# Up projections of three feed-forward stages as pairs of 64-row products into two banks

## The chip, the cores and the metric

One core of one Trainium2 chip runs the whole kernel, one launch. The metric is the device time in microseconds. Engines are named as in the profile: PE is TensorE's matrix multiply, PEld its weight load, DVE is VectorE, ACT is ScalarE, POOL is GpSimd, SP is SyncE.

## The reference

The kernel computes two transformer blocks on 256 tokens of width 1024, batch 1. The part that the change touches is the feed-forward half step, which occurs four times:

```python
def swiglu_half_step(h, g, w1, w3, w2):
    u = rmsnorm(h, g)
    return h + FFN_HALF * ((jax.nn.silu(u @ w1) * (u @ w3)) @ w2)
```

Here `w1` and `w3` are 1024 by 2816 and `w2` is 2816 by 1024, all float32. Between these steps lie a Mamba-2 mixer, a sliding-window attention, and a second block with an RWKV and latent-attention mixer and a mixture of experts.

## The kernel before

The stages run one after the other: `ffn0`, `ssm`, `ffn1`, `ffn2`, `kv`, `attn`, `ffn3`, `rwkv`, `mla`, `mix`, `peer`. Each engine has its own instruction list, and semaphores order them.

**How a product is made.** Weights come as tiles of 128 by 1024 floats through four ring slots (`ring`). For each tile ACT writes `w_hi`, the tile rounded to float32r (`make_hi`, L304), and DVE writes `w_lo`, the remainder (`make_lo`, L309). The normed activations are held in the same way as `u_hi` and `u_lo`. A product is then three float32r passes, hi by hi, hi by lo and lo by hi (`passes`, L357), summed in PSUM. `project_split` does this over the `DC` = 8 chunks of the contraction: each matmul has a 128 by 128 piece of the weights as its stationary operand and 256 token columns as its moving operand, so one product is 24 matmuls.

**A feed-forward stage** has `FC` = 22 hidden chunks of 128. They are taken alternately as `b` = 0 and 1. For every chunk `up` makes two products, with `w1` and with `w3`, into the two halves of bank `UP[b]` (banks 4 and 5). ACT then does `silu` on the first half (L695), and DVE does `gate` (L717 to L720): two multiplications of silu by the second half of the bank, and a subtraction that gives `x_hi` and `x_lo`. `down` (`close_split`) multiplies `x_hi` and `x_lo` by the `w2` tile into the four accumulators `ACC` (banks 0 to 3), in 12 matmuls with 512 moving columns.

**Order on PE.** The first chunk's products are made by `project_first`, which isn't changed. After `clear_acc` a loop of ten iterations does `up(1, i)`, `down(0, i)`, `up(0, i + 1)`, `down(1, i)`, and behind the loop come `up(1)` of the last chunk, then three quarters of `down(0)`, three of `down(1)`, and the last quarter of each. So an up of chunk j+1 always runs before the down of chunk j, and the gate of chunk j has the down of j-1 and the up of j+1 as its cover. Only at the end is this otherwise: the last chunk's gate has only three quarters of one down.

**Order on ACT and DVE.** In an iteration ACT does `silu` of a chunk and then three `make_hi` (the next `w1`, `w3` and `w2` tiles, in that order), and DVE does `gate` and then three `make_lo`. Each of these waits for the semaphore of what it needs, in the order of the list. Behind the loop DVE does `gate(0)`, `make_lo` of the last `w2` tile, `lead_next` (the `make_lo` of the first tile of the next stage) and `gate(1)`.

**Banks 6 and 7** are `TP[0]` and `TP[1]`. The stages' norms turn their rows through them. In `ffn2`, named `HOLDS_KV`, they also serve the key and value work; in `ffn0`, `ffn1` and `ffn3` they are idle during the loop.

Other code that the prediction reads in the trace: L386 (`project`, plain float32 with 128 rows and 256 columns), L1255 and L1256 (`scores`: for each half `a` of the partitions, rows 0 to 63 or 64 to 127, one product of 128 and one of 256 columns, each half into a bank of its own), L1542 (`lora`: four products on rows 0 to 63, then four on rows 64 to 127) and L1590 (`tile64`: alternating 64 by 64 products on the two halves). All of these are plain float32, and the profile lists each of their matmuls as two records. A float32r matmul is one record.

Of the kernel before, what the change touches and what calls it, by code (L numbers as in the profile page):

```python
# [31 lines left out]
P = 128  # L32
# [173 lines left out]
def program(nc, io, stages=STAGES):  # L206
# [23 lines left out]
    def S(name):  # L230
        if name not in sems:
            sems[name] = ctx.enter_context(nc.semaphore(name))
        return sems[name]
# [4 lines left out]
    with ctx:  # L238
# [31 lines left out]
        def area(at, *shape):  # L270

            n = int(np.prod(shape))
            a = arena[:, at:at + n]
            if len(shape) == 2:
                a = a.rearrange("p (a b) -> p a b", a=shape[0])
            if len(shape) == 3:
                a = a.rearrange("p (a b c) -> p a b c", a=shape[0], b=shape[1])
            return a
# [22 lines left out]
        def make_hi(act, slot, stage, i, nth=0):  # L301
            act.wait_ge(full[slot], (use(stage, slot, i, nth) + 1) * 16)
            act.wait_ge(split_read[slot], use_split(stage, slot, i, nth) + 1)
            act.activation(w_hi[slot][:, :], ring[slot][:, :], ACT.Copy).then_inc(hi_made[slot], 1)  # L304

        def make_lo(dve, slot, stage, i, nth=0):

            dve.wait_ge(hi_made[slot], use_split(stage, slot, i, nth) + 1)
            dve.tensor_tensor(w_lo[slot][:, :], ring[slot][:, :], w_hi[slot][:, :].bitcast(F32),  # L309
                              ALU.subtract).then_inc(freed[slot], 1)  # L310
# [10 lines left out]
        def lead_next(dve, before):  # L321

            for stage in stages[stages.index(before) + 1:][:1]:
                lead_vector(dve, stage, slice(0, 1))

        def lead_next_hi(act, before):

            for stage in stages[stages.index(before) + 1:][:1]:
                lead_scalar(act, stage, slice(0, LEAD_BEFORE.get(stage, 0)))
# [20 lines left out]
        def split_done(eng, slot, stage, i, nth=0):  # L350

            eng.wait_ge(split_read[slot], use_split(stage, slot, i, nth) + 2)
# [8 lines left out]
        def project_split(pe, out, slot, stage, i, nth=0):  # L361
            multiplied(pe, slot, stage, i, nth)
            for c in range(DC):
                cols = slice(c * P, (c + 1) * P)
                mm = passes(pe, out, (w_hi[slot][:, cols], w_lo[slot][:, cols]), (u_hi[:, c, :], u_lo[:, c, :]),
                            c == 0, c == DC - 1)
            return mm.then_inc(split_read[slot], 1)

        def close_split(pe, b, slot, stage, i, last=False, quarters=range(4)):

            multiplied(pe, slot, stage, i)
            for q in quarters:
                rows, cols = slice((q // 2) * P, (q // 2 + 1) * P), slice((q % 2) * 512, (q % 2 + 1) * 512)
                mm = passes(pe, ACC[q][:, :], (x_hi[:, b, rows], x_lo[:, b, rows]),
                            (w_hi[slot][:, cols], w_lo[slot][:, cols]), False, last)
                if last and q < 3:
                    mm.then_inc(S("acc_done"), 1)
            if q == 3:
                mm.then_inc(split_read[slot], 1)
# [233 lines left out]

        silu_buf = area(4 * D, 2, T)
        hid_buf = area(4 * D + 2 * T, 2, T)

        def stage_of(k):
            return f"ffn{k}"  # L620
# [9 lines left out]
        def ffn_tile(kind, k, i, b):  # L630
            return (2 + b, f"ffn{k}", i, 0) if kind == 2 else (kind, f"ffn{k}", i, b)
# [21 lines left out]
        def ffn_tensor(pe, k, updates):  # L653
            stage = f"ffn{k}"
            base = FC * ffn_no[stage]

            def up(b, i):
                pe.wait_ge(S("hid_ready"), base + 2 * i + b + 1)
                for n in range(2):
                    project_split(pe, UP[b][:, n * T:(n + 1) * T], *ffn_tile(n, k, i, b))  # L660

            def down(b, i, last=False, quarters=range(4)):
                pe.wait_ge(S("hid_ready"), base + 2 * i + b + 3)
                close_split(pe, b, 2 + b, stage, i, last, quarters)

            pe.wait_ge(S("hid_ready"), base + 1)
            project_first(pe, stage, *((UP[0][:, n * T:(n + 1) * T], *ffn_tile(n, k, 0, 0)) for n in range(2)), one_bank=True)
            clear_acc(pe, updates)
            if stage == HOLDS_KV:
                pe.wait_ge(S("table_loaded"), 16)  # L670
                pe.wait_ge(S("rest_loaded"), 16)
                pe.matmul(TP[0][0:16, 0:384], rel[0:BUCKETS, :], C("onehot")[0:BUCKETS, :], start=True,
                          stop=True).then_inc(S("line_done"), 1)
            with pe.Fori(0, FC // 2 - 1) as i:
                up(1, i)
                down(0, i)
                up(0, i + 1)
                down(1, i)
            up(1, FC // 2 - 1)
            if stage == HOLDS_KV:  # L680
                pe.wait_ge(S("line_ready"), 1)
                kv_turn(pe, 0)
                kv_turn(pe, 1)
            down(0, FC // 2 - 1, quarters=range(3))
            if stage == HOLDS_KV:
                kv_turn(pe, 2)
                kv_turn(pe, 3)
            down(1, FC // 2 - 1, True, range(3))
            down(0, FC // 2 - 1, quarters=(3,))
            down(1, FC // 2 - 1, True, (3,))  # L690

        def ffn_scalar(act, k):
            def silu(b, i):
                split_done(act, *ffn_tile(1, k, i, b))
                act.activation(silu_buf[:, b, :], UP[b][:, 0:T], ACT.Silu).then_inc(S("silu_ready"), 1)  # L695

            act.preload_act_table(ACT.Silu)
            for kind in range(2):
                make_hi(act, *ffn_tile(kind, k, 0, 1))
            with act.Fori(0, FC // 2 - 1) as i:  # L700
                for b in range(2):
                    silu(b, i)
                    for kind, *at in ffn_next(k, i, b):
                        make_hi(act, *ffn_tile(kind, k, *at))
            silu(0, FC // 2 - 1)
            make_hi(act, *ffn_tile(2, k, FC // 2 - 1, 1))
            lead_next_hi(act, stage_of(k))
            silu(1, FC // 2 - 1)

        def ffn_vector(dve, k):  # L710
            stage = f"ffn{k}"
            base = FC * ffn_no[stage]

            def gate(b, i):
                dve.wait_ge(S("silu_ready"), base + 2 * i + b + 1)
                dve.wait_ge(split_read[2 + b], use_split(stage, 2 + b, i) + 1)
                dve.tensor_tensor(x_hi[:, b, :], silu_buf[:, b, :], UP[b][:, T:2 * T], ALU.mult)  # L717
                dve.tensor_tensor(hid_buf[:, b, :], silu_buf[:, b, :], UP[b][:, T:2 * T], ALU.mult)
                dve.drain()
                dve.tensor_tensor(x_lo[:, b, :], hid_buf[:, b, :], x_hi[:, b, :].bitcast(F32),  # L720
                                  ALU.subtract).then_inc(S("hid_ready"), 1)

            for kind in range(2):
                make_lo(dve, *ffn_tile(kind, k, 0, 1))
            if stage == HOLDS_KV:
                dve.wait_ge(S("line_done"), 1)
                dve.tensor_tensor(bias_line[0:16, :], TP[0][0:16, 0:384], C("outside")[0:16, :],
                                  ALU.add).then_inc(S("line_ready"), 1)
            with dve.Fori(0, FC // 2 - 1) as i:
                for b in range(2):  # L730
                    gate(b, i)
                    for kind, *at in ffn_next(k, i, b):
                        make_lo(dve, *ffn_tile(kind, k, *at))
            gate(0, FC // 2 - 1)
            make_lo(dve, *ffn_tile(2, k, FC // 2 - 1, 1))
            lead_next(dve, stage)
            gate(1, FC // 2 - 1)
            if stage == HOLDS_KV:
                for q in range(4):
                    dve.wait_ge(S("kv_turned"), q + 1)  # L740
                    dve.tensor_tensor(quarter(u_t, q), TP[q % 2][:, :].rearrange("p (c t) -> p c t", c=4),
                                      spread(V("g_kv", 4 * (q % 2), 4 * (q % 2) + 4), P), ALU.mult).then_inc(S("kv_made"), 1)
            update_h(dve, 0.5, upd[stage], stage)
# [2401 lines left out]
```

## Time and profile before

| | us |
|---|---|
| median of 2 runs | 2172.53 |
| lowest and highest | 2172.39, 2172.67 |
| profiled execution, its own time | 2173.42 |
| its span in the trace | 2171.2 |
| PE busy | 2133.1 (98%) |
| PEld busy | 1923.5 (89%) |
| DVE busy | 1450.1 (67%) |
| ACT busy | 1039.8 (48%) |

The trace's durations are summed against the span. The time of a run is about 2 us more than the span of the same execution (2173.42 against 2171.2), which lies around it, and the median is 0.9 us below the profiled execution.

A matmul's record lasts longer than the matmul keeps the array, since records overlap: what a stream of matmuls costs is the distance from one start to the next, got here by dividing a stretch by the count in it. "64*128 64x256" in a row is a product with 64 rows (contraction) and 128 stationary columns, whose moving operand is 64 by 256.

### The profile page before, as it was taken

What the parts mean: (1) busy time and instruction counts of PE and PEld (TensorE: products, weight loads), DVE (VectorE), ACT (ScalarE), POOL (GpSimd) and SP (SyncE); (2) the same over time, 40 slices, a digit from 0 to 9 for tenths busy, and PEclk for the clock granted to TensorE, in tenths of its full rate; (3) what the DMA queues carried; (4) which work ended last, traced back from release to release, by engine and by line L of the source; (5) the groups of instructions that cost most, each with busy time, mean ns of one, the idle gap of its engine ahead of it and who ended that gap; (6) DMA issues with size and microseconds to landing.
All of it is one profiled execution on the core that took longest, in us unless ns stands there. A gap on an engine that the chain in (4) does not pass through costs nothing.

```text
span 2171.2 us, 41978 instructions
## 1 busy us (share of the span) xinstructions
PE 2133.1 (98%) x15291; PEld 1923.5 (89%) x15291; DVE 1450.1 (67%) x2757; ACT 1039.8 (48%) x1766; POOL 104.0 (5%) x78
## 2 busy tenths in 40 slices
PE   9999999999999999999999899999999999999999
PEld 7999998899899987899899669889889999999998
DVE  5556998555565546655685578989886666666665
ACT  4335776433444336533562464458534444444443
POOL 0000000000000000000000004500000000000000
PEclk9999999999999999999999999999999999999999
DMA  6555664455566534455541034344677666665664
GB/s 216 186 187 173 206 194 134 159 187 188 174 207 207 189 131 131 166 188 186 184 146 54 21 117 147 117 169 146 212 228 237 207 204 204 210 185 185 190 185 135
DMA packets 107724, 374.23 MB, mean 172 GB/s; under 512 B 11984, under 2 KB 17888, under 8 KB 107376
## 3 DMA queue, kind: packets, MB, share of 16 engines
q1 hardware_dynamic: 102848, 355.01, 50.1%
q0 software_dynamic: 4784, 17.99, 2.8%
q8 instruction: 58, 0.95, 0.2%
q14 instruction: 34, 0.28, 0.0%
HBM read 362.41 MB, written 13.69 MB: 173 GB/s over the span
## 4 chain that ended last, share of the span: by engine, by line
PE 88%; DVE 6%; ACT 2%; DVEq 1%; DMA 1%; issue 1%; POOL 0%; ACTq 0%
PE bank L357 71%; PE bank L386 5%; PE bank L1590 3%; PE bank L2650 2%; DVE w_lo L309 1%; PE bank L563 1%; ACT w_hi L304 1%; DVE arena L2836 0%; DVE arena L2829 0%; PE bank L581 0%; PE bank L339 0%; DMA ring<-in_ssm_in 0%; DVE arena L2830 0%; PE bank L341 0%; PE bank L2174 0%
## 5 line engine op out<-in xcount | busy, mean ns | idle before, releaser
L309 DVE TENSOR_TENSOR w_lo<-ring,w_hi 128x1024 fp32r<-128x1024 f32 x575 | 695.0, 1222 | 410.9 <-ACT w_hi L304 408.9
L304 ACT ACTIVATE w_hi<-ring 128x1024 fp32r<-128x1024 f32 x599 | 624.6, 1056 | 631.1 <-PE bank L357 568.9
L357 PE MATMUL bank<-u_hi,w_hi 128*128 128x256 f32 x2712 | 771.4, 284 | 7.2 <-POOL w_lo L309 5.3
L357 PE MATMUL bank<-u_hi,w_lo 128*128 128x256 f32 x2712 | 767.4, 283 | 0.0
L357 PE MATMUL bank<-u_lo,w_hi 128*128 128x256 f32 x2712 | 767.3, 283 | 0.0
L357 PEld LDWEIGHTS bank<-u_hi,w_hi 128*128 128x128 f32 x2712 | 519.7, 192 | 19.3 <-issue 8.0
L357 PEld LDWEIGHTS bank<-u_lo,w_hi 128*128 128x128 f32 x2712 | 519.7, 192 | 7.5 <-issue 0.5
L357 PEld LDWEIGHTS bank<-u_hi,w_lo 128*128 128x128 f32 x2712 | 519.7, 192 | 0.0
L357 PE MATMUL bank<-w_hi,x_hi 128*128 128x512 f32 x992 | 390.8, 394 | 1.3 <-DVE x_lo L2158 0.9
L357 PE MATMUL bank<-w_lo,x_hi 128*128 128x512 f32 x992 | 388.3, 391 | 0.0
L357 PE MATMUL bank<-w_hi,x_lo 128*128 128x512 f32 x992 | 386.1, 389 | 0.0
L357 PEld LDWEIGHTS bank<-w_hi,x_lo 128*128 128x128 f32 x992 | 186.3, 188 | 40.5
L357 PEld LDWEIGHTS bank<-w_hi,x_hi 128*128 128x128 f32 x992 | 187.0, 188 | 39.2 <-DVE x_lo L2158 1.8
L357 PEld LDWEIGHTS bank<-w_lo,x_hi 128*128 128x128 f32 x992 | 187.0, 189 | 31.3
L386 PE MATMUL bank<-u_t,ring 128*128 128x256 f32 x640 | 145.3, 382 | 0.9 <-DVE u_t L520 0.7
L386 PEld LDWEIGHTS bank<-u_t,ring 128*128 128x128 f32 x640 | 119.6, 191 | 19.0 <-issue 1.3
L2901 DVE TENSOR_TENSOR x_hi<-arena 128x256 fp32r<-128x256 f32 (+1 forms) x128 | 54.4, 425 | 121.8 <-ACT arena L2745 111.4
L2745 ACT ACTIVATE arena<-bank 128x256 f32<-128x256 f32 x96 | 37.1, 386 | 176.8 <-PE bank L357 176.8
L309 POOL TENSOR_TENSOR w_lo<-ring,w_hi 128x1024 fp32r<-128x1024 f32 x24 | 56.9, 2384 | 1103.5 <-ACT w_hi L304 1095.5
L2650 PE MATMUL bank<-arena 128*128 128x128 f32 x512 | 63.1, 278 | 2.7 <-issue 1.7
L2650 PEld LDWEIGHTS bank<-arena 128*128 128x128 f32 x512 | 60.5, 191 | 5.8 <-issue 2.6
L1590 PE MATMUL bank<-arena 64*64 64x64 f32 (+1 forms) x1504 | 55.6, 228 | 7.1 <-ACT arena L1824 2.6
(316 smaller groups left out, 1793.5 us busy)
## 6 DMA issues: line engine op xcount, KB each, us to landing
ring<-in_w SPq DMA_DIRECT2D x264, 512.0 KB, 3.6
ring<-in_expert_u SPq DMA_DIRECT2D x128, 512.0 KB, 3.5
ring<-in_expert_v SPq DMA_DIRECT2D x128, 512.0 KB, 4.1
ring<-in_ssm_in SPq DMA_DIRECT2D x40, 512.0 KB, 4.3
gate_dram<-con SPq DMA_DIRECT2D x16, 576.0 KB, 2.8
arena<-gate_dram POOLq DMA_DIRECT2D x9, 1024.0 KB, 8.5
ring<-in_ssm_out SPq DMA_DIRECT2D x16, 512.0 KB, 4.2
ring<-in_w_o SPq DMA_DIRECT2D x16, 512.0 KB, 3.6
```

Source lines behind the costliest of these rows:

```text
L304: act.activation(w_hi[slot][:, :], ring[slot][:, :], ACT.Copy).then_inc(hi_made[slot], 1)
L309: dve.tensor_tensor(w_lo[slot][:, :], ring[slot][:, :], w_hi[slot][:, :].bitcast(F32), ALU.subtract).then_inc(freed[slot], 1)
L357: mm = pe.matmul(out, left[a], right[b], start=start and n == 0, stop=stop and n == 2, skip_group_check=True)
L386: mm = pe.matmul(out, ring[slot][:, c * width:(c + 1) * width], u_t[:, c, :], start=(c == 0), stop=(c == DC - 1))
L563: pe.matmul(bank[4][:, :], zeros[:, 0:P], zeros[:, :], start=True, stop=True)
L1590: mm = pe.matmul(bank[b][a, at:at + width], left[a, :], right[a, :], start=(n == 0), stop=(n == len(products) - 1))
L2650: mm = pe.matmul(ROT[g][:, t * P:(t + 1) * P], one_b[:, g, t, :], one_a[:, g, t, :], start=True, stop=True)
L2745: act.activation(gelu_buf[:, n, :], ROT[n][:, 0:T], ACT.Gelu).then_inc(S("gelu_out"), 1)
L2901: dve.tensor_tensor(chunks(x_hi[:, n:n + 1, :]), chunks(src), gates, ALU.mult)
```

## The change

`project_rows` takes the place of `project_split` in `up` for the stages `ffn0`, `ffn1` and `ffn3` (`IN_ROWS`). Each 128-row matmul becomes two with 64 rows: rows 0 to 63 of weights and activations into `UP[b]`, rows 64 to 127 into `TP[b]`. The two halves of a sum then lie in two banks. ACT copies `TP[b]` to `up_sum` in SBUF (`keep_half`), DVE adds `UP[b]` to it (`add_rows`), and `silu` and `gate` read `up_sum` in place of the bank. The first chunk, still made by `project_first`, is copied whole by DVE (`first=True`).

```diff
@@ project_split is followed by:
+        def project_rows(pe, outs, slot, stage, i, nth=0):
+            multiplied(pe, slot, stage, i, nth)
+            for c in range(DC):
+                cols = slice(c * P, (c + 1) * P)
+                for n, (a, b) in enumerate(((0, 0), (0, 1), (1, 0))):
+                    for out, rows in zip(outs, (slice(0, HD), slice(HD, P))):
+                        mm = pe.matmul(out, (w_hi, w_lo)[a][slot][rows, cols], (u_hi, u_lo)[b][rows, c, :],
+                                       start=c == 0 and n == 0, stop=c == DC - 1 and n == 2, skip_group_check=True)
+            return mm.then_inc(split_read[slot], 1)
...
+        up_sum = area(8400, 2, 2 * T)
+        IN_ROWS = [k for k in range(4) if f"ffn{k}" != HOLDS_KV]
...
             def up(b, i):
                 pe.wait_ge(S("hid_ready"), base + 2 * i + b + 1)
                 for n in range(2):
-                    project_split(pe, UP[b][:, n * T:(n + 1) * T], *ffn_tile(n, k, i, b))
+                    cols = slice(n * T, (n + 1) * T)
+                    if k in IN_ROWS:
+                        project_rows(pe, (UP[b][:, cols], TP[b][:, cols]), *ffn_tile(n, k, i, b))
+                    else:
+                        project_split(pe, UP[b][:, cols], *ffn_tile(n, k, i, b))
...
         def ffn_scalar(act, k):
+            def keep_half(b, i):
+                if k in IN_ROWS:
+                    split_done(act, *ffn_tile(1, k, i, b))
+                    act.activation(up_sum[:, b, :], TP[b][:, :], ACT.Copy).then_inc(S("up_summed"), 1)
+
             def silu(b, i):
-                split_done(act, *ffn_tile(1, k, i, b))
-                act.activation(silu_buf[:, b, :], UP[b][:, 0:T], ACT.Silu).then_inc(S("silu_ready"), 1)
+                if k in IN_ROWS:
+                    act.wait_ge(S("up_summed"), 2 * FC * IN_ROWS.index(k) + 4 * i + 2 * b + 2)
+                    src = up_sum[:, b, :]
+                else:
+                    split_done(act, *ffn_tile(1, k, i, b))
+                    src = UP[b]
+                act.activation(silu_buf[:, b, :], src[:, 0:T], ACT.Silu).then_inc(S("silu_ready"), 1)
...
                     silu(b, i)
                     for kind, *at in ffn_next(k, i, b):
                         make_hi(act, *ffn_tile(kind, k, *at))
+                    keep_half(1 - b, i + b)
             silu(0, FC // 2 - 1)
             make_hi(act, *ffn_tile(2, k, FC // 2 - 1, 1))
             lead_next_hi(act, stage_of(k))
+            keep_half(1, FC // 2 - 1)
             silu(1, FC // 2 - 1)
...
+            def add_rows(b, i, first=False):
+                if k not in IN_ROWS:
+                    return
+                if first:
+                    split_done(dve, *ffn_tile(1, k, i, b))
+                    dve.tensor_copy(up_sum[:, b, :], UP[b][:, :]).then_inc(S("up_summed"), 2)
+                else:
+                    dve.wait_ge(S("up_summed"), 2 * FC * IN_ROWS.index(k) + 4 * i + 2 * b + 1)
+                    dve.tensor_tensor(up_sum[:, b, :], up_sum[:, b, :], UP[b][:, :], ALU.add).then_inc(S("up_summed"), 1)
+
             def gate(b, i):
+                src = up_sum[:, b, :] if k in IN_ROWS else UP[b]
...
             for kind in range(2):
                 make_lo(dve, *ffn_tile(kind, k, 0, 1))
+            add_rows(0, 0, first=True)
...
                     gate(b, i)
                     for kind, *at in ffn_next(k, i, b):
                         make_lo(dve, *ffn_tile(kind, k, *at))
+                    add_rows(1 - b, i + b)
             gate(0, FC // 2 - 1)
             make_lo(dve, *ffn_tile(2, k, FC // 2 - 1, 1))
+            add_rows(1, FC // 2 - 1)
             lead_next(dve, stage)
             gate(1, FC // 2 - 1)
```

In `gate` both multiplications read `src[:, T:2 * T]` in place of `UP[b][:, T:2 * T]`.

## Rows read from the trace of the kernel before

**Rows 1.** The chain that ended last: shares by engine, then its longest pieces.
```profile
PE 88%; DVE 6%; ACT 2%; DVEq 1%; DMA 1%; issue 1%; POOL 0%; ACTq 0%
...
21.07 181.50 PE bank L357 x1272
...
897.98 181.51 PE bank L357 x1272
```

**Rows 2.** Busy time by stretch: one down, then one up, in ffn0.
```profile
core 0: us, PE busy (x) PEld busy (x) DVE busy (x) ACT busy (x) POOL busy (x), PEclk, DMA share, GB/s
26.92:29.66 2.74, 2.74 (x14) 2.26 (x13) 1.54 (x3) 2.28 (x3) 0.00 (x0) 1.00 0.48 151
29.66:35.42 5.76, 5.76 (x50) 5.75 (x48) 3.28 (x5) 1.06 (x1) 0.00 (x0) 1.00 0.57 217
```

**Rows 3.** Timeline, PE: the steady stream of an up, 128-row float32r matmuls.
```profile
300.27 0.28 PE L357 MATMUL bank<-u_lo,w_hi 128*128 128x256 f32 x1
300.39 0.28 PE L357 MATMUL bank<-u_hi,w_lo 128*128 128x256 f32 x1
```

**Rows 4.** Timeline, chain and source view: 64-row pairs, and plain float32 with 128 rows.
```profile
824.99 0.61 PE L1256 MATMUL bank<-arena 64*128 64x256 f32 x4
...
1406.40 3.47 PE bank L386 x16
...
L1256 PE MATMUL bank<-arena x32: 376/377/378, 809.9 to 857.2; 64*128 64x256 f32 x32
```

**Rows 5.** Timeline, PE, where 64-row and 128-row products meet.
```profile
1149.84 0.28 PE L357 MATMUL bank<-u_hi,w_lo 128*128 128x256 f32 x1
1150.05 2.08 PE L1590 MATMUL bank<-arena 64*64 64x64 f32 x64
1152.06 0.39 PE L357 MATMUL bank<-u_hi,w_hi 128*128 128x256 f32 x1
1152.28 0.28 PE L357 MATMUL bank<-u_lo,w_hi 128*128 128x256 f32 x1
...
1099.61 2.96 PE L1542 MATMUL bank<-arena 64*128 64x256 f32 x16 [0.60 <-ACT arena L1785]
1102.51 0.39 PE L357 MATMUL bank<-u_hi,w_hi 128*128 128x256 f32 x1
1102.73 0.28 PE L357 MATMUL bank<-u_lo,w_hi 128*128 128x256 f32 x1
...
823.71 1.03 PE L386 MATMUL bank<-u_t,ring 128*128 128x256 f32 x4
824.67 0.50 PE L1255 MATMUL bank<-arena 64*128 64x128 f32 x4
```

**Rows 6.** Timeline, ACT then DVE, over one chunk of ffn0.
```profile
29.09 0.36 ACT L695 ACTIVATE arena<-bank 128x256 f32<-128x256 f32 x1
...
28.27 2.36 DVE L309 TENSOR_TENSOR w_lo<-ring,w_hi 128x1024 fp32r<-128x1024 f32 x2 [1.20 <-ACT w_hi L304]
...
31.37 0.43 DVE L720 TENSOR_TENSOR x_lo<-arena,x_hi 128x256 fp32r<-128x256 f32 x1
...
33.89 1.23 DVE L309 TENSOR_TENSOR w_lo<-ring,w_hi 128x1024 fp32r<-128x1024 f32 x1 [2.10 <-ACT w_hi L304]
```

**Rows 7.** Timeline: the end of ffn0, then one operation each of 512 columns.
```profile
195.39 1.23 DVE L309 TENSOR_TENSOR w_lo<-ring,w_hi 128x1024 fp32r<-128x1024 f32 x1 [0.96 <-ACT w_hi L304]
...
197.12 0.39 ACT L695 ACTIVATE arena<-bank 128x256 f32<-128x256 f32 x1 [1.76 <-PE bank L357]
...
198.37 0.43 DVE L720 TENSOR_TENSOR x_lo<-arena,x_hi 128x256 fp32r<-128x256 f32 x1
...
198.98 0.40 PE L357 MATMUL bank<-w_hi,x_hi 128*128 128x512 f32 x1
...
202.91 0.61 ACT L475 ACTIVATE arena<-h 128x512 f32<-128x512 f32 x1
...
204.78 0.69 DVE L520 TENSOR_TENSOR u_hi<-bank,vec 128x512 fp32r<-128x512 f32 x1 [0.70 <-PE bank L581]
```

More of the change, by code:

```diff
@@ L712, in ffn_vector @@
             base = FC * ffn_no[stage]
+            def add_rows(b, i, first=False):
[7 more added lines that the diff above has]
+                    dve.tensor_tensor(up_sum[:, b, :], up_sum[:, b, :], UP[b][:, :], ALU.add).then_inc(S("up_summed"), 1)
             def gate(b, i):
+                src = up_sum[:, b, :] if k in IN_ROWS else UP[b]
                 dve.wait_ge(S("silu_ready"), base + 2 * i + b + 1)
                 dve.wait_ge(split_read[2 + b], use_split(stage, 2 + b, i) + 1)
-                dve.tensor_tensor(x_hi[:, b, :], silu_buf[:, b, :], UP[b][:, T:2 * T], ALU.mult)
-                dve.tensor_tensor(hid_buf[:, b, :], silu_buf[:, b, :], UP[b][:, T:2 * T], ALU.mult)
+                dve.tensor_tensor(x_hi[:, b, :], silu_buf[:, b, :], src[:, T:2 * T], ALU.mult)
+                dve.tensor_tensor(hid_buf[:, b, :], silu_buf[:, b, :], src[:, T:2 * T], ALU.mult)
                 dve.drain()
```

## The prediction

> **What bounds the kernel now.** I read first the page's chain of work that ended last. PE holds 88% of it, and each changed stage appears there as one unbroken piece of L357 of 181.5 us; the rows show ffn0 and ffn3, the first and last of three such pieces [rows 1]. So within these stages nothing but the rate of matmuls counts, and a microsecond put on PE's list is a microsecond of the kernel.
>
> Next the busy time by stretch. One down is 2.74 us for 12 matmuls of 512 columns, 0.228 us each, and one up is 5.76 us for 48 matmuls of 256 columns, 0.120 us each; the granted clock is 1.00 in both, the 2.4 GHz level. Weight loads are busy through 5.75 of the up's 5.76 us, hidden under the stream. DVE is busy for 1.54 + 3.28 = 4.82 us of the 8.50 us of one chunk and ACT for 2.28 + 1.06 = 3.34 [rows 2]. The timeline gives the same 0.12 us between two starts [rows 3]. From the two sizes a matmul costs (0.228 - 0.120) = 0.108 us per 256 columns and 0.012 us besides, whatever its length. That 0.012 us is all that a better arrangement of an up could win, since the columns to be streamed remain.
>
> **PE, the streams.** Each stage does 21 ups by the new way (the first of 22 chunks stays with `project_first`): 21 x 48 x 3 = 3024 matmuls of 128 rows become 3024 pairs of 64 rows. Everything hangs on what a pair costs.
>
> Do two halves of the array run side by side? L1256 shows four records of 64 rows and 256 columns, two for each half, done in 0.61 us, a record lasting 0.377. L386, plain float32 on 128 rows, starts one every 3.47 / 16 = 0.217 us; at that distance four in a row would take 3 x 0.217 + 0.377 = 1.03 us. One such distance and one duration are 0.59. So the halves do run together, each at the pace of a full-height stream [rows 4]. Nor is the issue of instructions in the way: L1590 gets 64 records, each with its load, through in 2.08 us, so at most 2.08 / 64 = 0.033 us each [rows 5]; a pair needs two in 0.120.
>
> All these are plain float32, which takes 0.217 us for 256 columns, half the pace of float32r. No row has two float32r streams at once. Bounds: below, a pair costs its columns alone, 0.108, if the 0.012 vanishes (-36 us over 3024 pairs); above, each of the two loads costs its own 0.012, 0.132 per pair (+36); far above, the float32r streams don't overlap, 2 x 0.120 (+363). I take 0.120, change zero, since in plain float32 two halves neither gained nor lost against one full stream, which is the nearest row.
>
> The Trainium skill (TensorE: Matmul & The Clock Gate, Part 3, The mechanism) says that a weight load overlaps matmuls in flight only where their row groups differ. The trace disagrees for the present up: loads busy for 5.75 of 5.76 us with a matmul every 0.120, where 107 ns of load laid bare, an estimate from the page's LDWEIGHTS figure, would make some 0.21. By this rule the pairs would be the better form, at best 0.108.
>
> **PE, the seams.** Ups would run in 64-row form, downs stay at 128 rows, so each of 63 ups is entered and left by a change of form. Such changes are in the trace. Entering: an L357 record at 1149.84, the next form at 1150.05, 0.21 us instead of 0.12; and L386's last record begins at 823.71 + 1.03 - 0.377 = 824.36, L1255 at 824.67, 0.31 instead of 0.217. So 0.09 us of waiting. In addition the first load is no longer hidden. Leaving shows both: L1542's last record begins at 1099.61 + 2.96 - 0.377 = 1102.19, L357 at 1102.51 (0.32 instead of 0.217, 0.10 more), its second at 1102.73 (0.22 instead of 0.12, 0.10 more); L1590 to L357 has the same 0.22 at 1152.06 [rows 4, 5]. One seam is 0.10 + 0.10, taken as 0.19 with the shorter entry. Seams: 63 x 2 x 0.19 = **23.9 us**, straight on PE's list. Below, only the wait, 126 x 0.09 = 11.3; above, 126 x 0.22 = 27.7.
>
> The Trainium skill (TensorEngine Tiling (Array Packing), Tiling Modes, Key Properties) says that changing the tiling mode drains the engine. The trace has this and the exposed load behind it; by the drain alone, at the 0.09 us of the rows, the seams would be 11.3 us.
>
> **ACT and DVE in the loop.** New per chunk: a copy of 128x512 on ACT, near L475's 0.61 us, and a 128x512 addition on DVE reading one bank, as L520 does in 0.69 [rows 7]. ACT goes to 3.95, DVE to 5.51 us of a chunk that is then 8.88 long. What matters is when the gate ends. Up ended at 26.92, the start of the down [rows 2]; silu runs at 29.09, the two `make_lo` end at 30.63 and the gate at 31.80; the next down needs it at 35.42 [rows 2, 6]. Now: copy 29.09 to 29.70, addition 30.63 to 31.32, silu (0.36) to 31.68, gate 1.29 (as at the end of the stage, below) to 32.97. PE has 2.5 us to spare, and more by the seams. The next `make_lo` on DVE began at 33.89 [rows 6], so nothing queued behind the gate is late, nor a ring slot freed later. Cost 0. Were the cover gone, it would be 0.69 + 0.61 = 1.3 us per chunk, 82 us over 63; a faster pair (up in 5.18) still leaves some 1.9. The sync list and its DMAs aren't touched: the same tiles, freed by the same `make_lo`. The extra 0.69 us of DVE for the first chunk's copy stands before a gate that has a whole up as cover.
>
> **The end of each stage.** Here the cover is short. The last silu runs from 197.12 to 197.51, the gate ends at 198.80, 1.29 us on, and the last down begins at 198.98: 0.18 us to spare [rows 7]. `lead_next`'s `make_lo` ran at 195.39, before the last up was done; now `add_rows` stands in front of it on DVE's list and waits for ACT's copy, so it too comes after. New order: copy 197.12 to 197.73, addition to 198.42, `make_lo` (1.23) to 199.65, gate 1.29 to 200.94, while PE, behind the seam at 196.9, is ready at 198.98 + 0.19 = 199.17. PE waits 1.77 us, in three stages 1.77 x 3 = **5.3 us**. The normalisation behind it starts from the accumulators and moves with them. Bounds: 0 if DVE had all to hand, 7 if ACT's table load falls badly.
>
> **The sum.** 0 + 23.9 + 0 + 5.3 = +29.2 us. Against the profiled span 2171.2 that is 2200.4; against the median 2172.5, **2201.7 us**, +1.3%.
>
> **The rivals.**
> *Loads cost double* (20%). Each half's load holds up float32r reads for 0.012 us in both halves: 0.132 per pair. For it: the 0.012 is the same at 256 and 512 columns, as a price per load would be, and plain float32, at half the pace, hides it (0.217 is 2 x 0.108 with nothing over). Against it: the halves read different partitions. 2201.7 + 36.3 = 2238, slower than before by 3.0%. It decides as soon as a pair costs over 0.125, where 2% is passed (43.4 - 29.2 = 14.2 us over 3024).
> *The 0.012 goes* (12%). Two streams fill each other's gaps: 0.108 per pair, 2201.7 - 36.3 = 2165, 0.3% faster; this is also how the skill's rule on loads would come out. Against it: each half has its own stream with its own loads, and nothing in [rows 4] got shorter.
> *float32r streams don't overlap* (8%): both halves wait for one read path that plain float32 uses only half. 2201.7 + 363 = 2565. No row excludes it.
> *PE is late with instructions* (8%): twice as many, four in 0.120 us and a loop body almost twice as long. L1590's pace speaks against it. At 0.126 to 0.130 per pair, 2220 to 2232.
> The forecast itself has 52%.
>
> **How the numbers follow.** The predicted time is the forecast's. The range takes in both bounds of the load's price and of the seams: 2164 below, 2242 above; outside lie the streams that don't overlap and what I haven't thought of. The forecast's own range, with pairs of 0.118 to 0.123 and the seams' bounds, is 2183 to 2214. Two per cent, about what a measurement of this kernel can tell from no change, is 43.4 us, so 2129 and 2216. Slower by over 2%: 20 + 8 + about 6 of the 8 = 34%. Faster: even 0.108 with free seams and no wait at the ends gives 2136, so 3%. Within: 63%.
>
> **What the new profile would show.** A chunk of 8.50 us would be 8.88, the piece of 181.5 us about 191. An up would be about 5.76 us with 96 records, starts in pairs a few ns apart and pairs 0.120 apart; this decides between the first three cases. Entry and exit show starts of 0.2 us more and a second start late by 0.1. At 197 to 201 of ffn0 PE idles for 1.7 us, released by DVE's `x_lo`. ffn2 keeps its times. Wrong it would be made by a pair far from 0.120, or by seams that cost something else between float32r products than between plain ones.

## The result and the profile after

| | before | after |
|---|---|---|
| median, us | 2172.53 | 2201.35 |
| lowest and highest | 2172.39, 2172.67 | 2201.18, 2201.51 |
| span of the profiled execution | 2171.2 | 2199.7 |
| matmul records (PE) | 15291 | 18301 |

The ratio is 1.0131, with a 95% interval of 1.0114 to 1.0147: slower by 28.8 us, clear of noise and within 2%. The forecast was 2201.7. The new products add 3024 matmuls, so 18315 records would be right; 14 are missing from the trace.

The busy time by stretch of the changed kernel, for the down and the up that answer to [rows 2]:

```profile
core 0: us, PE busy (x) PEld busy (x) DVE busy (x) ACT busy (x) POOL busy (x), PEclk, DMA share, GB/s
26.82:29.76 2.94, 2.94 (x14) 2.17 (x12) 1.35 (x3) 2.22 (x3) 0.00 (x0) 1.00 0.71 226
29.76:35.70 5.94, 5.94 (x98) 5.81 (x97) 4.18 (x6) 1.87 (x3) 0.00 (x0) 1.00 0.59 194
```

The down went from 2.74 to 2.94 us and the up from 5.76 to 5.94. PE is busy through all of it, with nearly twice the records in the up. A chunk takes 8.88 us in place of 8.50, as forecast.

The timeline of PE, first where a down ends and an up begins, then in the steady part, then where the up ends ("x2" is one product of each half of the rows, listed as one line because the two start within 4 ns):

```profile
29.22 0.39 PE L357 MATMUL bank<-w_lo,x_hi 128*128 128x512 f32 x1
29.44 0.39 PE L357 MATMUL bank<-w_hi,x_lo 128*128 128x512 f32 x1
29.76 0.38 PE L375 MATMUL bank<-u_hi,w_hi 64*128 64x256 f32 x2
29.98 0.28 PE L375 MATMUL bank<-u_lo,w_hi 64*128 64x256 f32 x2
30.10 0.28 PE L375 MATMUL bank<-u_hi,w_lo 64*128 64x256 f32 x2
...
35.49 0.28 PE L375 MATMUL bank<-u_hi,w_lo 64*128 64x256 f32 x2
35.70 0.50 PE L357 MATMUL bank<-w_hi,x_hi 128*128 128x512 f32 x1
36.04 0.40 PE L357 MATMUL bank<-w_lo,x_hi 128*128 128x512 f32 x1
```

Pairs start 0.12 us apart, as single matmuls did in [rows 3]. At the entry the first pair starts 0.32 us after the last matmul of the down, where 0.23 is the ordinary distance, and the second pair 0.22 after the first instead of 0.12. At the exit the distances are 0.21 instead of 0.12, then 0.34 instead of 0.23. These four excesses, some 0.09, 0.10, 0.09 and 0.11, make 0.39 us per up; the starts are read to 0.01 us each, and the chunk's length, the better measure, gives 0.38.

That the second excess of each pair is a weight load no longer hidden can be read from PEld, for the last up of ffn0, before and then after. Before, the load for the down's first product starts 0.12 us ahead of it; after, with it:

```profile
196.80 0.19 PEld L357 LDWEIGHTS bank<-w_hi,x_hi 128*128 128x128 f32 x1
196.92 0.40 PE L357 MATMUL bank<-w_hi,x_hi 128*128 128x512 f32 x1
```

```profile
204.42 0.19 PEld L357 LDWEIGHTS bank<-w_hi,x_hi 128*128 128x128 f32 x1
204.42 0.50 PE L357 MATMUL bank<-w_hi,x_hi 128*128 128x512 f32 x1
```

The end of ffn0, from the timeline of ACT, DVE and PE, which answers to [rows 7]:

```profile
204.53 0.60 ACT L712 ACTIVATE arena<-bank 128x512 f32<-128x512 f32 x1 [1.75 <-PE bank L375]
...
205.16 0.69 DVE L750 TENSOR_TENSOR arena<-arena,bank 128x512 f32<-128x512 f32 x1 [2.52 <-ACT arena L712]
...
205.77 1.22 DVE L309 TENSOR_TENSOR w_lo<-ring,w_hi 128x1024 fp32r<-128x1024 f32 x1
205.88 0.42 ACT L721 ACTIVATE arena<-arena 128x256 f32<-128x256 f32 x1 [0.76 <-DVE arena L750]
...
206.36 0.39 PE L357 MATMUL bank<-w_hi,x_lo 128*128 128x512 f32 x1
206.90 0.42 DVE L756 TENSOR_TENSOR x_hi<-arena 128x256 fp32r<-128x256 f32 x1
...
207.73 0.42 DVE L759 TENSOR_TENSOR x_lo<-arena,x_hi 128x256 fp32r<-128x256 f32 x1
208.21 0.50 PE L357 MATMUL bank<-w_hi,x_hi 128*128 128x512 f32 x1 [1.46 <-DVE x_lo L759]
...
208.55 0.40 PE L357 MATMUL bank<-w_lo,x_hi 128*128 128x512 f32 x1
```

Copy, addition, the next stage's `make_lo` and the gate run one after the other, and PE starts the last down 208.21 - 206.36 = 1.85 us after its predecessor instead of 0.23: 1.62 us lost. After the wait the first load is bare too, so the second product starts 0.34 us after the first instead of 0.23, another 0.11. Each of the three stages loses these 1.73 us.

### The profile page after: what moved, and what is told of

It is laid out like the page before. It is cut to its first block, busy times and chain, and to the rows that moved or that the text cites. A ratio compares the mean times of both kernels' runs of the same rounds, so it can differ in the third digit from the quotient of the medians.

```text
span 2199.7 us, 48234 instructions
## 1 busy us (share of the span) xinstructions
PE 2156.3 (98%) x18301; PEld 1922.1 (87%) x18315; DVE 1495.8 (68%) x2823; ACT 1080.6 (49%) x1829; POOL 104.0 (5%) x78
## 4 chain that ended last, share of the span: by engine, by line
PE 89%; DVE 6%; ACT 2%; DVEq 1%; issue 1%; DMA 1%; POOL 0%; ACTq 0%
PE bank L357 55%; PE bank L375 17%; PE bank L396 5%; PE bank L1632 3%; PE bank L2692 2%; DVE w_lo L309 1%; PE bank L573 1%; PE bank L339 1%; PE bank L341 0%; DVE arena L2878 0%; DVE arena L2871 0%; ACT w_hi L304 0%; PE bank L591 0%; DVE arena L2872 0%; PE bank L346 0%
## 5 line engine op out<-in xcount | busy, mean ns | idle before, releaser
L357 PE MATMUL bank<-u_hi,w_hi 128*128 128x256 f32 x1704 | 486.1, 285 | 4.6 <-POOL w_lo L309 4.6
L357 PE MATMUL bank<-u_hi,w_lo 128*128 128x256 f32 x1704 | 482.1, 283 | 0.0
L357 PE MATMUL bank<-u_lo,w_hi 128*128 128x256 f32 x1704 | 482.1, 283 | 0.0
L357 PEld LDWEIGHTS bank<-u_hi,w_hi 128*128 128x128 f32 x1704 | 326.4, 192 | 13.0 <-issue 7.3
L357 PEld LDWEIGHTS bank<-u_lo,w_hi 128*128 128x128 f32 x1704 | 326.4, 192 | 5.2 <-issue 0.5
L357 PEld LDWEIGHTS bank<-u_hi,w_lo 128*128 128x128 f32 x1704 | 326.4, 192 | 0.0
L375 PE MATMUL bank<-u_hi,w_hi 64*128 64x256 f32 x2016 | 291.9, 286 | 1.9 <-DVE w_lo L309 1.9
L375 PE MATMUL bank<-u_lo,w_hi 64*128 64x256 f32 x2016 | 285.4, 280 | 0.0
L375 PE MATMUL bank<-u_hi,w_lo 64*128 64x256 f32 x2016 | 285.1, 279 | 0.0
L375 PEld LDWEIGHTS bank<-u_lo,w_hi 64*128 64x128 f32 x2016 | 192.0, 187 | 0.0
```

Source lines behind the costliest of these rows:

```text
L357: mm = pe.matmul(out, left[a], right[b], start=start and n == 0, stop=stop and n == 2, skip_group_check=True)
L375: mm = pe.matmul(out, (w_hi, w_lo)[a][slot][rows, cols], (u_hi, u_lo)[b][rows, c, :], start=c == 0 and n == 0, stop=c == DC - 1 and n == 2 ...
```

## The length of ffn1, run by run

To keep the other stages out of the comparison, the table takes the stretch from the end of `ssm` to the end of `ffn1`, where PE's list has a group of products of zeros (`keep_busy`) that shows in every timeline. Before, the chain of work has the groups at 397.42 and 591.30 us, 193.88 apart; after, they stand like this in the timeline:

```profile
406.55 1.67 PE L573 MATMUL bank<-zeros 128*128 128x512 bf16 x7
...
609.97 1.67 PE L573 MATMUL bank<-zeros 128*128 128x512 bf16 x7
```

In `after` and in e5 to e8 the first record of the group is missing (x7), at both ends of the stretch, so its length stays right to 0.01 us.

| run | ffn1 stretch, us | against before | one chunk, us |
|---|---|---|---|
| before | 193.88 | | 8.50 |
| after | 203.42 | +9.54 | 8.88 |
| e1, PE alone | 201.66 | +7.78 | 8.88 |
| e2, ACT and DVE alone | 195.82 | +1.94 | 8.50 |
| e3, half the pairs | 203.43 | +9.55 | 8.86 |
| e4, half the pairs, twice the seams | 210.88 | +17.00 | 9.23 |
| e5, one dummy product | 200.60 | +6.72 | 8.82 |
| e6, last chunk as before | 201.31 | +7.43 | 8.88 |
| e7, blocks of three | 201.80 | +7.92 | 8.89 |
| e8, blocks of 24 | 298.40 | +104.52 | 13.49 |

"One chunk" is the distance from the start of a down to the start of the next in ffn0. Three stages at 9.6, 9.5 and 9.6 us make 28.7 us, where the span grew by 28.5: what the other stages gained and lost nearly cancels (see the last section).

## Experiments: which part costs

**e1.** The kernel before with the new products on PE, and nothing changed on ACT and DVE:

```diff
+        def project_rows(pe, outs, slot, stage, i, nth=0):   # as in the change
...
+                    if k in IN_ROWS:
+                        project_rows(pe, (UP[b][:, cols], TP[b][:, cols]), *ffn_tile(n, k, i, b))
```

> The kernel before with project_rows on PE alone: ACT and DVE as before. The sums of rows 64 to 127 are made in TP and read by nobody, so the hidden activations leave half of the contraction out. Theory (seams): 63 ups x 2 changes of form x 0.19 us = 23.9 us and nothing at the ends of the stages: 2196.4 us, period of a chunk 8.88 us. Rival (ACT and DVE hold PE up): close to 2172.5.

Measured: 2196.85 us, ratio 1.0108 (1.0091 to 1.0125). A chunk takes 8.88 us.

**e2.** The other half of the change, with ups of 128 rows as before (on PE, `up` calls `project_split` in every stage):

```diff
-                    if k in IN_ROWS:
-                        project_rows(pe, (UP[b][:, cols], TP[b][:, cols]), *ffn_tile(n, k, i, b))
-                    else:
+                    if True:
...
-                    act.activation(up_sum[:, b, :], TP[b][:, :], ACT.Copy).then_inc(S("up_summed"), 1)
+                    act.activation(up_sum[:, b, :], UP[b][:, :], ACT.Copy).then_inc(S("up_summed"), 1)
...
-                    dve.tensor_tensor(up_sum[:, b, :], up_sum[:, b, :], UP[b][:, :], ALU.add)
+                    dve.tensor_tensor(up_sum[:, b, :], up_sum[:, b, :], UP[b][:, :], ALU.max)
```

> The changed kernel with ups on PE as before, 128 rows into UP; ACT copies UP (not TP) to up_sum, and DVE takes the maximum of up_sum and UP in place of the sum, the same operation in size. Theory: hidden in the loop (period 8.50 us), only the three stage ends cost, 1.8 us each without a seam before them: 2172.5 + 5.4 = 2177.9 us. Rival (ACT and DVE are behind most of the 29 us): 2195 or more.

Measured: 2177.28 us, ratio 1.0017 (1.0007 to 1.0027), which makes 3.7 us, where three stages at the 1.94 us of ffn1 make 5.8; whole times are blurred by what the last section tells. The chunk keeps its 8.50 us, and the longest wait of PE in this run is at the ends of the three stages (the time counts only idle time between records, so it is less than the delay):

```profile
PE bank L357 <- DVE x_lo L757: 4.9, 3, 1.6
```

So PE's part is +7.78 us in ffn1 and that of ACT and DVE +1.94; together 9.72, where both at once cost 9.54. They add up but for 0.18: PE goes through the seam behind the last up while it would be waiting anyway, and waits that much less (1.85 us between the two starts after, 2.04 in e3, which has no seam there).

## Experiments: pairs or seams

**e3.** Half as many pairs, as many changes of form:

```diff
+            in_rows = (range(4, DC), range(0, 4))[slot]
             for c in range(DC):
...
+                if c not in in_rows:
+                    mm = passes(pe, outs[0], ...)
+                    continue
```

> The changed kernel with only half of the pairs and as many changes of form: w1's contraction chunks 4 to 7 and w3's chunks 0 to 3 in pairs, the rest 128 rows; one stretch of pairs in each up. Theory (seams only, a pair costs what a 128-row matmul does): the same as the changed kernel, 2201.4 us. Rival (each pair costs 0.008 us more, (28.8 - 4.9) / 3024, and a change of form nothing): 1512 pairs fewer, 12 us less, 2189 us.

**e4.** Half as many pairs, twice as many changes of form:

```diff
+            in_rows = range(0, 4)                       # the rest as in e3
```

> Half of the pairs as well, but chunks 0 to 3 in pairs and 4 to 7 in 128 rows in both products: four changes of form for each up in place of two, none between up and down. Theory (seams): 126 more changes x 0.19 us, 2201.4 + 23.9 = 2225.3 us. Rival (pairs): 2189 us, as with the run of half the pairs and one stretch.

Measured: e3 2198.37 us, ratio 1.0117 (1.01 to 1.0134); e4 2221.51 us, 1.0222 (1.0205 to 1.0239). Both came out 3 to 4 us under what the seams alone would make, and neither at the rival's 2189. e3's profiled span is 3.1 us shorter than the changed kernel's, and 2.7 of these lie between the end of ffn3 and the norm of `peer`, which neither run changes (see the last section). The chunk decides: 8.86 us in e3 against 8.88 with all pairs, where a price on the pairs would have made it the mean of 8.50 and 8.88, 8.69. That the stretch of ffn1 equals the changed kernel's to 0.01 us is partly chance: 21 x 0.02 us less in the loop, against 0.19 more at the end, where no seam behind the last up shortens the wait, and 0.19 for a first seam that is no longer hidden (below). e4 against e3 is 210.88 - 203.43 = 7.45 us for 42 more changes of form, 0.18 us each, and the same by the chunks, (9.23 - 8.86) / 2.

**e5.** A change of form alone, in the kernel before:

```diff
                     project_split(pe, UP[b][:, n * T:(n + 1) * T], *ffn_tile(n, k, i, b))
+                    if n == 0 and k in IN_ROWS:
+                        pe.matmul(TP[b][:, 0:HD], zeros[0:HD, 0:P], zeros[0:HD, 0:HD], start=True, stop=True)
```

> The kernel before with one 64-row product of zeros (bf16, 64 columns) between the two products of each up in ffn0, ffn1 and ffn3: two changes of form for each up and nothing else of the change. Theory (seams): entering 0.09 us of waiting and a short bf16 load, 0.03 of streaming, leaving 0.09 and 0.10 of a bare load: about 0.34 us x 63 = 21 us, 2194 us. Rival (a change of form costs nothing in a stream of float32r): 63 x 0.03, 2174.5 us.

Measured: 2193.07 us, ratio 1.0095 (1.0078 to 1.0112). The timeline of PE around the one product:

```profile
32.83 0.28 PE L357 MATMUL bank<-u_lo,w_hi 128*128 128x256 f32 x1
32.95 0.28 PE L357 MATMUL bank<-u_hi,w_lo 128*128 128x256 f32 x1
33.17 0.20 PE L663 MATMUL bank<-zeros 64*128 64x64 bf16 x1
33.30 0.39 PE L357 MATMUL bank<-u_hi,w_hi 128*128 128x256 f32 x1
33.52 0.28 PE L357 MATMUL bank<-u_lo,w_hi 128*128 128x256 f32 x1
```

From 32.95 to 33.52 are 0.57 us where two distances of 0.12 were: one product of 64 columns, with nothing to compute, costs 0.33 us here, 0.32 by the chunk, and 63 of them 20.2 us. That is 70% of the whole change's loss, with neither its pairs nor its additions.

The product differs from its neighbours in more than its rows: in type, in moving columns and in the bank it writes. The probes of e9 (below) settle which of these costs. Their bf16 products, 128 rows into another bank, lengthen the chunk of ffn0 to 11.13 us, by 2.63, which is 24 x 0.109 and nothing for two changes of type. Those of 64 stationary columns are entered and left without an excess:

```profile
509.25 0.39 PE L357 MATMUL bank<-w_hi,x_lo 128*128 128x512 f32 x1
509.48 0.28 PE L379 MATMUL bank<-u_hi,w_hi 128*64 128x256 f32 x1
509.59 0.28 PE L379 MATMUL bank<-u_lo,w_hi 128*64 128x256 f32 x1
...
512.09 0.28 PE L379 MATMUL bank<-u_hi,w_lo 128*64 128x256 f32 x1
512.20 0.28 PE L357 MATMUL bank<-u_hi,w_hi 128*128 128x256 f32 x1
```

Only the probes with 64 rows show the seam: in e9's ffn3 they start 0.32 us after the down's last product instead of 0.23, with their second start 0.22 later. So it is the change in rows that costs.

**e6.** The changed kernel without the wait at the ends (`old=True` takes the code of before; the semaphore counts follow):

```diff
-            up(1, FC // 2 - 1)
+            up(1, FC // 2 - 1, old=True)
...
-            keep_half(1, FC // 2 - 1)
-            silu(1, FC // 2 - 1)
+            silu(1, FC // 2 - 1, old=True)
...
-            add_rows(1, FC // 2 - 1)
             lead_next(dve, stage)
-            gate(1, FC // 2 - 1)
+            gate(1, FC // 2 - 1, old=True)
```

> The changed kernel with the last chunk of each stage as before: 128 rows into UP, silu and gate read the bank, no copy and no addition between them. Theory: the wait of 1.62 us at each end goes, and with it two changes of form a stage: 2201.4 - 3 x 1.62 - 6 x 0.19 = 2195.4 us. Rival (the wait at the end is covered by the normalisation behind it, and comes back there): 2200.3 us.

Measured: 2193.43 us, ratio 1.0096 (1.0079 to 1.0112). The stretch of ffn1 is 2.11 us shorter than in the changed kernel, and the wait, the bare load behind it and one up's seams make 1.62 + 0.11 + 0.38 = 2.11; the `x_lo` of the ups has left the waits of PE. The wait isn't given back by the normalisation behind it: the stretch that follows ffn1 takes 292.7 us in both. By the whole times the gain looks larger, 7.9 us where three stages make 6.3; in the profiled spans it is 8.7, and 1.7 of that lies between ffn3 and the norm of `peer`, which the edit doesn't touch (last section).

## Experiments: how two halves run together

**e7, e8.** PE alone, in another order:

```diff
-                for n, (a, b) in enumerate(((0, 0), (0, 1), (1, 0))):
-                    for out, rows in zip(outs, (slice(0, HD), slice(HD, P))):
+            for c0 in range(0, DC, BLOCK):          # BLOCK = 1 in e7, 8 in e8
+                for out, rows in zip(outs, (slice(0, HD), slice(HD, P))):
+                    for c in range(c0, c0 + BLOCK):
...
+                        for n, (a, b) in enumerate(((0, 0), (0, 1), (1, 0))):
```

> As the run of PE alone (half of the contraction left out of the hidden activations), but three products of the lower half, then three of the upper half, in place of alternating. Theory (the idle half may start some instructions ahead in the list, as in L1542, where the upper half began while the lower was in its third of four): the halves still overlap, close to PE alone, 2196. Rival (the halves start only in list order, one instruction ahead): the overlap is one of three, up to 3024 x 0.12 x 2/3 = 240 us more.

> As the run of PE alone (half of the contraction left out), but all 24 products of the lower half, then all 24 of the upper half. Theory (a few instructions of look-ahead): two or three of 24 overlap at each change of half, so a product takes about 24 + 20 distances of 0.12 in place of 24: 126 x 20 x 0.12 = 300 us more than PE alone, about 2500 us. Without any overlap 2196 + 363 = 2559 us; with deep look-ahead 2196.

Measured, one execution each: e7 2197.91 us, e8 2488.49. The timeline of e8 where the lower half's 24 products end and the upper half's begin:

```profile
37.04 0.28 PE L376 MATMUL bank<-u_hi,w_lo 64*128 64x256 f32 x1
37.05 0.39 PE L376 MATMUL bank<-u_hi,w_hi 64*128 64x256 f32 x2
37.27 0.29 PE L376 MATMUL bank<-u_lo,w_hi 64*128 64x256 f32 x2
37.39 0.29 PE L376 MATMUL bank<-u_hi,w_lo 64*128 64x256 f32 x2
37.50 0.28 PE L376 MATMUL bank<-u_hi,w_hi 64*128 64x256 f32 x1
```

The upper half starts at 37.05, when the lower one still has three to start, and they run side by side (x2) for these three; then it goes on alone, one each 0.12. Its own first load is bare, so its second product starts 0.22 us after its first. Over the stage e8 costs (104.52 - 7.78) / 42 = 2.30 us per product more than e1, 19 distances of 0.12, so what overlaps is worth about 5 of 24, at two changes of half: three at each, less the 0.10 us of the late second start. In blocks of three nothing is lost but 0.006 us per chunk (0.14 us over the stage). Here a free half started three products ahead in the list, and not 24.

**e9, e10.** Where the 0.012 us of each float32r matmul comes from. 24 products that nobody reads (in e10's ffn0 and ffn3 24 pairs) were put ahead of each up of the kernel before, another kind in each stage:

```diff
+                        pe.matmul(tp[:, 0:T], w[...].bitcast(BF16)[:, 0:P], u.bitcast(BF16)[:, 0:T], ...)   # ffn0, e9
+                        pe.matmul(tp[0:HD, 0:T], w[:, c * P:c * P + HD], u, ...)                            # ffn1, e9
+                        pe.matmul(tp[:, 0:T], w[low, c * P:(c + 1) * P], u[low, :], ...)                    # ffn3, e9
...
+                            pe.matmul(out[:, 0:T], w[rows, ...].bitcast(BF16)[:, 0:P], u[rows, :].bitcast(BF16)[:, 0:T], ...)   # ffn0, e10
+                        pe.matmul(tp[:, 0:P], w[:, c * P:(c + 1) * P], u[:, 0:P], ...)                # ffn1, e10
+                            pe.matmul(out[:, 0:P], w[rows, c * P:(c + 1) * P], u[rows, 0:P], ...)     # ffn3, e10
```

> The kernel before with 24 products that nobody reads at the start of each up, to read the distance between two starts where a 128-row float32r matmul of 256 columns has 0.120 us: in ffn0 with bf16 operands of the same shape, in ffn1 float32r with 64 stationary columns (half the weight load), in ffn3 float32r on rows 0 to 63 alone. Theory A (the 0.012 us is the reading of float32r weights beside a float32r stream, and follows the size of the load): about 0.108, 0.114 and 0.120. Theory B (it is a fixed part of each float32r matmul): about 0.108, 0.120 and 0.120.

> As the probe of one stream, with other products: in ffn0 24 pairs of 64-row bf16 products, in ffn1 float32r with 128 rows and 128 moving columns, in ffn3 24 float32r pairs of 64 rows and 128 moving columns. Theory (each half is a stream of its own, and pays as one full stream does): bf16 pairs 0.108; 128 columns 0.112 to 0.117, since there the weight load alone takes about 0.11; pairs of 128 columns the same again. Rival (two halves share something that the 256-column float32r pairs just don't exhaust, such as starts of instructions or weight reads): pairs of 128 columns dearer than one 128-row matmul of 128 columns.

Measured, one execution each: e9 2350.74 us, e10 2352.39; what counts are the distances. The timelines give them by the second and the last of 24, 22 distances. In e9, bf16 and then 64 stationary columns:

```profile
65.58 0.27 PE L377 MATMUL bank<-u_lo,w_hi 128*128 128x256 bf16 x1
...
67.98 0.27 PE L377 MATMUL bank<-u_hi,w_lo 128*128 128x256 bf16 x1
...
509.59 0.28 PE L379 MATMUL bank<-u_lo,w_hi 128*64 128x256 f32 x1
...
512.09 0.28 PE L379 MATMUL bank<-u_hi,w_lo 128*64 128x256 f32 x1
```

and in e10, pairs of bf16 and then pairs of float32r with 128 columns:

```profile
66.97 0.27 PE L378 MATMUL bank<-u_lo,w_hi 64*128 64x256 bf16 x2
...
69.37 0.27 PE L378 MATMUL bank<-u_hi,w_lo 64*128 64x256 bf16 x2
...
1049.60 0.28 PE L380 MATMUL bank<-u_lo,w_hi 64*128 64x128 f32 x2
...
1052.06 0.28 PE L380 MATMUL bank<-u_hi,w_lo 64*128 64x128 f32 x2
```

| stationary by moving | distance, us |
|---|---|
| float32r, 128 rows, 128 by 256 (the ups before) | 0.120 |
| float32r pairs, 64 rows, 128 by 256 (the change) | 0.120 |
| float32r, 64 rows alone, 128 by 256 | 0.120 |
| float32r, 128 rows, 64 by 256 | 0.114 |
| bf16, 128 rows, 128 by 256 | 0.109 |
| bf16 pairs, 64 rows, 128 by 256 | 0.109 |
| float32r, 128 rows, 128 by 128 | 0.112 |
| float32r pairs, 64 rows, 128 by 128 | 0.112 |

Half the load's columns take away half of what float32r costs over bf16 (0.120, 0.114, 0.109). That speaks for theory A, a weight load that holds up the stream beside it in proportion to its size, and against a fixed part of every float32r matmul, as the prediction had it ("whatever its length"). The probe halves the output's partitions along with the load, so the two aren't told apart; and why the price arises (which read waits for which) isn't shown. In each kind a pair of 64 rows costs just what one product of 128 rows costs, which fits halves that carry each their own stream and loads, and pay the load's price at the same time. With half the moving columns the distance falls only to 0.112, for one as for two. That the load of 128 columns sets the pace there was the reason for expecting it, and no run here shows it by itself.

## Why the prediction was right

*A pair costs what one matmul did (0).* Right: 0.120 us, by the timeline, and by e3, where half of the pairs taken away changed the chunk by 0.02 us. The argument from plain float32, that two halves neither gain nor lose against one full stream, carried over to a pace twice as high. Of the rivals, *loads cost double* (0.132) and *the 0.012 goes* (0.108) are both ruled out by the 0.120: by e9 and e10 the price seems to go with the load, but two halves don't pay it one after the other, nor does either fill the other's gap. *Streams don't overlap* would have been e8's way: it shows what the change costs if a half has no partner, 2488 us, though even there overlap is worth five of 24. *PE is late with instructions* leaves no trace in the ups: pairs of bf16 run at 0.109.

The Trainium skill (TensorE: Matmul & The Clock Gate, Part 3, The mechanism) has weight loads overlap matmuls in flight only across row groups. No run here agrees: one stream on one half alone, with 128 columns to load for each product, starts one every 0.120 us, as with two halves.

*Seams (23.9).* Right in size, 0.38 us per up by the chunk's length, and right in kind: what plain float32 showed, a wait and a bare load at each change, holds for float32r. By the stage it is 7.78 us (e1), not 21 x 0.38 = 7.98: PE's first up in a stage waits for DVE's `w_lo` anyway, and its first load is bare anyway. Before, it started at 409.80 after 0.64 us of idle time and its second product 0.22 later; in e1 at 418.58 after 0.63, and the second again 0.22 later. So the first entry of each stage costs nothing, and 41 seams of 0.19 make the 7.78. In three stages that is 23.3 us. The waits of PE after:

```profile
PE bank L375 <- DVE w_lo L309: 1.9, 3, 0.6
```

e5 shows the seam by itself, e4 that it is the number of seams that counts, and e9 that it takes a change in rows.

*ACT and DVE in the loop (0).* Right: e2 has 8.50 us per chunk. The gate ended at 33.27 us where the forecast said 32.97, with the down at 35.70, and the timeline of ACT and DVE shows why: the addition starts at 30.84, 0.2 us later than in the working, and silu reading SBUF takes 0.42 us, not 0.36 as from the bank.

```profile
29.57 0.58 ACT L712 ACTIVATE arena<-bank 128x512 f32<-128x512 f32 x1
31.56 0.42 ACT L721 ACTIVATE arena<-arena 128x256 f32<-128x256 f32 x1 [1.41 <-DVE arena L750]
...
30.84 0.68 DVE L750 TENSOR_TENSOR arena<-arena,bank 128x512 f32<-128x512 f32 x1
32.01 0.42 DVE L756 TENSOR_TENSOR x_hi<-arena 128x256 fp32r<-128x256 f32 x1 [0.49 <-ACT arena L721]
32.84 0.43 DVE L759 TENSOR_TENSOR x_lo<-arena,x_hi 128x256 fp32r<-128x256 f32 x1
```

*The ends (5.3).* 3 x 1.73 = 5.2 us, but made up otherwise. The wait is 1.62 us and not 1.77: the durations were right, but operations that follow each other on one engine overlap by some 0.1 us in the records (205.77 + 1.22 = 206.99, and the next began at 206.90), and the working added them whole. The 0.11 us of the bare load behind the wait wasn't in the working. That the two errors nearly cancel is luck.

*The sum.* 29.2 forecast, 28.7 in the three stages and 28.8 by the medians. That the whole times agree as well as the stages is luck: the other stages lost 1.6 us to a spell of lower clock in the profile before, and 2.0 us, which the forecast put at nothing, between ffn3 and `peer` in the profile after (last section).

*The range.* Its lower end, 2164, was said to take in the lower bound of the seams; it doesn't. With 0.108 per pair and 11.3 us of seams the sum is 2172.5 - 36.3 + 11.3 + 5.3 = 2152.8. The upper end, 2242, is as worked out.

## What to carry to other kernels

Splitting a full-height contraction into two row halves wins nothing on TensorE: two half-height streams together run at the pace of one full stream, load price included, and a second product is free only where a half was empty (one 64-row product alone took 0.120 us, a pair of them 0.120). Count the places where PE's list goes from 128 rows to 64 or back, and price each at the wait plus the first load that is no longer hidden (0.19 us here); a single tiny product of the other form in a dense stream costs two of them, 0.33 us. When work is added in front of a gate, look at the last iteration, where the cover that the loop gives is gone.

## What was not expected of the hardware

The profiled executions differ outside the changed stages, for two reasons. The first is a spell of lower granted clock, a short time at the 1.2 GHz level; it fell in `attn` before and in `rwkv` after, places that the change doesn't touch. The busy time by stretch, before and then after; the first number behind POOL is the granted clock:

```profile
815.00:835.00 20.00, 18.10 (x112) 13.93 (x111) 12.72 (x47) 12.28 (x44) 0.00 (x0) 0.91 0.44 125
```

```profile
1205.00:1215.00 10.00, 8.01 (x206) 7.76 (x207) 6.16 (x18) 1.68 (x3) 0.00 (x0) 0.83 0.07 25
```

PE was not fully busy in either (18.1 of 20 us, 8.0 of 10). From the end of ffn1 to the norm of ffn3 the kernel before took 294.29 us, and the changed kernel, e2, e3 and e4, without a spell there, 292.7: the spell was worth 1.6 us.

The second is a wait of PE. From the end of ffn3 to the norm of `peer` the changed kernel took 219.77 us and e3 217.10, and of these 2.67 us only some 0.8 are the spell's. The other 1.84 had come up before it, when PE stood still in `rwkv` for 1.7 us for nothing that the profile shows ("issue"). e1, whose stretch of 218.73 us has no spell, has the wait too. The waits of PE after, and then in e1:

```profile
PE bank L1632 <- issue: 1.7, 1, 1.7
```

```profile
PE bank L1605 <- issue: 1.4, 1, 1.4
```

It is there in the five kernels whose new ups are 64-row products throughout (after, e1, e6, e7 and e8; 0.7 us in e6, 1.4 to 1.7 in the others), nearly gone in e4 (0.2) and absent in the other six. So up to 1.7 us of the 28.8 may be a cost of the change that neither the prediction nor the table of ffn1 has. Twice as many instructions in PE's loop is a guess at the cause; no run isolates it. The kernel before, with 217.80 us, has in its place a wait of 0.60 us for ACT at the start of the stretch ([rows 5], L1542), which the changed kernel lacks.

So a comparison to 1 us needs the stretch of the changed stage, not the span: by the spans e3 would be 3.1 us faster than the changed kernel, and in none of its changed stages is it faster by more than 0.1.
